# Depthwise convolution by phases: three half-length filters, all four chunks on GpSimd, in a hybrid decoder step on one core

## The reference

```
h = h + 0.5 * SwiGLU_1(rms(h))
n = rms(h);  z = n @ w_in
A: latent attention, 8 heads (prompt: causal; samples: 2048 cached positions in pages)
B: v = u1 * sigmoid(u2)                                        # 512 channels, GLU
   c[t] = conv_b + sum over x = 0..30 of conv_w[x] * v_ext[t + x]   # per channel
   c = silu(layernorm over channels (c))
h = h + concat(A, c) @ w_o
h = h + 0.5 * SwiGLU_2(rms(h))
h = h + sigmoid(rms(h) @ w_pg + b_pg) * (p @ w_pp)
y = rms(h)
```

## Time and profile before

| | |
|---|---|
| median of 3 runs | 2373.71 us (2373.28 to 2376.27) |
| the profiled execution's own time | 2374.75 us |
| its span, first to last instruction | 2372.9 us |
| busy, share of the span | PE 94%, DVE 52%, ACT 25%, POOL 13% |
| mean granted TensorE clock | 0.975 of full speed |

### The profile page before, as it was taken

One profiled execution on the slowest core, in us unless ns is written; L12 is line 12 of the kernel. 1 busy time (PEld: TensorE's weight loads), 2 busy tenths in 40 slices (PEclk: granted clock), 3 DMA queues, 4 the chain that ended last, 5 costly groups with the idle time before them and its releaser, 6 DMA issues.

```text
span 2372.9 us, 36251 instructions
## 1 busy us (share of the span) xinstructions
PE 2235.9 (94%) x14234; PEld 2099.8 (88%) x14234; DVE 1236.1 (52%) x1940; ACT 599.9 (25%) x967; POOL 308.4 (13%) x173
## 2 busy tenths in 40 slices
PE   6999999999999999968888899999999999999897
PEld 5999999999999999735544689999999999999796
DVE  7444444444445725457678546544444444445746
ACT  6211111111112314232342433211111111112423
POOL 0000000000000000799995000000000000000000
PEclk9999999999999999878999999999999999999899
DMA  4111111111111330374343311111111111111202
GB/s 149 45 45 44 44 35 53 53 53 37 50 36 36 131 108 9 102 117 123 113 123 114 110 54 54 36 45 44 39 50 53 53 44 45 35 53 36 80 19 73
DMA packets 97113, 150.84 MB, mean 64 GB/s; under 512 B 12113, under 2 KB 73970, under 8 KB 96610
## 3 DMA queue, kind: packets, MB, share of 16 engines
q1 hardware_dynamic: 96098, 140.49, 19.9%
q0 software_dynamic: 928, 9.17, 1.1%
HBM read 139.21 MB, written 10.42 MB: 63 GB/s over the span
## 4 chain that ended last, share of the span: by engine, by line
PE 81%; DVE 10%; ACT 4%; SPq 2%; issue 2%; DMA 1%; DVEq 0%; ACTq 0%
PE ps L469 25%; PE ps L470 24%; PE ps L471 24%; DVE cacc L1525 2%; PE ps L714 2%; PE ps L671 1%; DVE stat L1628 1%; SPq L322 1%; ACT sq L886 1%; SPq L329 1%; PE ps L729 1%; PE ps L739 1%; DVE n L1278 1%; DVE wlo L1251 1%; PE ps L629 1%
## 5 line engine op out<-in xcount | busy, mean ns | idle before, releaser
L469 PE MATMUL ps<-n_hi,wlo 128*128 128x352 f32 x2832 | 922.8, 326 | 21.6 <-DVE wlo L1251 13.7
L471 PE MATMUL ps<-n_hi,whi 128*128 128x352 f32 x2832 | 911.3, 322 | 0.0
L470 PE MATMUL ps<-n_lo,whi 128*128 128x352 f32 x2832 | 910.9, 322 | 0.0
L469 PEld LDWEIGHTS ps<-n_hi,wlo 128*128 128x128 f32 x2832 | 533.9, 189 | 26.1 <-issue 14.4
L470 PEld LDWEIGHTS ps<-n_lo,whi 128*128 128x128 f32 x2832 | 535.4, 189 | 2.0 <-issue 0.2
L471 PEld LDWEIGHTS ps<-n_hi,whi 128*128 128x128 f32 x2832 | 533.7, 188 | 0.0
L469 PE MATMUL ps<-hid_hi,wlo 128*128 128x352 f32 x1104 | 359.7, 326 | 25.1 <-DVE h L1306 12.1
L470 PE MATMUL ps<-hid_lo,whi 128*128 128x352 f32 x1104 | 355.5, 322 | 0.0
L471 PE MATMUL ps<-hid_hi,whi 128*128 128x352 f32 x1104 | 355.4, 322 | 0.0
L1306 DVE SCALAR_TENSOR_TENSOR h<-ps,h 128x352 f32<-128x352 f32 x552 | 273.1, 520 | 153.1 <-PE ps L471 153.1
L1319 DVE TENSOR_TENSOR gact<-ps,rstd 128x352 f32<-128x352 f32 x132 | 69.1, 523 | 530.9 <-PE ps L471 530.9
(11 more groups left out here) (182 smaller groups left out, 1546.0 us busy)
## 6 DMA issues: line engine op xcount, KB each, us to landing
raw<-in_wstream SPq DMA_DIRECT2D x167, 512.0 KB, 3.6
ttile<-in_cacheT SPq DMA_DIRECT2D x128, 144.0 KB, 2.6
ctile<-in_cache SPq DMA_DIRECT2D x128, 128.0 KB, 2.0
out_yT<-h POOLq DMA_DIRECT2D x1, 4224.0 KB, 13.7
h<-out_yT SPq DMA_DIRECT2D x3, 1408.0 KB, 11.5
out_yT<-n SPq DMA_DIRECT2D x2, 1408.0 KB, 5.7
sw<-in_samplew POOLq DMA_DIRECT2D x1, 2560.0 KB, 10.2
pw<-in_pairw SPq DMA_DIRECT2D x4, 640.0 KB, 4.7
```

Of the source, the lines that this page charges most:

```text
L469: nc.tensor.matmul(out, w_l, x_h, start=first, stop=False)
L470: nc.tensor.matmul(out, w_h, x_l, start=False, stop=False)
L471: return nc.tensor.matmul(out, w_h, x_h, start=False, stop=last)
```

## The change

The prompt's convolution is computed by phases. `vext` and `cacc` keep even and odd positions apart. With E(w) the filter of the 16 even taps on the even positions, O(w) that of the 15 odd taps on the odd ones, and B that of the summed taps on the sum of both phases, the even outputs are E + O, and the odd ones B - E - O shifted by one position. So three filters of half as many positions and about half as many taps replace one of full length. GpSimd does this for all four chunks; VectorE does none of it. VectorE makes the summed taps (`wboth`) and doubled bias (`bias2`) once, and does the samples' convolution in pairs 0, 1, 1 and 2.

Scratch tiles lie in other tiles: the products of chunk 0 in `prod_n` (a part of `n_hi` that `att_high(1)` writes), those of the other chunks in `prod_v` (chunk 0 of `vext`), so GpSimd waits ahead of chunk 1 until SP has stored the prompt's convolution state. That store and the samples' ones move behind load round 5.

The sample queries move in TensorE's list from behind the last GLU tile to behind tile (3, 0), the absorbed ones to behind tile (3, 1); VectorE's scaling and ScalarE's copies move with them. SP loads the page table, the rotary table and the first pair's weights earlier, reads the page numbers of a round before it waits for the round's buffer, and takes the second round's `load_t` ahead of the first `load_c`. GLU, LayerNorm sums, centring and scaling use strided operands; `scale_rows(2)` comes ahead of `conv_low(0)`.

The core of the diff (tiles' places, semaphores and host code are cut):

```diff
-POOL_CHUNKS = (0, 1)
-SHARED, SHARED_DVE, DVE_CHUNK = 2, 17, 3
-POOL_STEPS = len(POOL_CHUNKS) * (2 * TAPS - 1) + 2 * (TAPS - SHARED_DVE)
+HALF = SEQ // 2
+HR, HB = ROWS // 2, RB // 2
+HH, HV = HIST // 2, (HIST + SEQ) // 2
+EVEN = (TAPS + 1) // 2
+FILTERS = [("odd", a) for a in range(1, EVEN)] + [("even", a) for a in range(EVEN)] + [("both", a) for a in range(EVEN)]
+POOL_CHUNK_STEPS = 1 + 2 * len(FILTERS) - 3 + 3
+POOL_STEPS = CC * POOL_CHUNK_STEPS
...
+    zq = scope()
+    phase_p = sb(zq, "phase_p", [P, HV])
+    odd_p = sb(zq, "odd_p", [P, HALF + 1])
+    zq.close()
...
-    vext = sb(zb, "vext", [P, CC, HIST + SEQ])
+    zv = scope()
+    prod_v = sb(zv, "prod_v", [P, HALF + 1])
+    zv.close()
+    vext = sb(zb, "vext", [P, CC, 2, HV])
...
+    prod_n = sb(zo, "prod_n", [P, ROWS])
+    terms_s = sb(zo, "terms_s", [P, ROWS])
...
+    cacc = sb(zo, "cacc", [P, CC, 2, HR])
...
-    product = sqs[:, :, :].rearrange("p c n -> p (c n)")
-
-    def tap_operands(c, x):
-        return (cacc[:, c, 0:SEQ], vext[:, c, x:x + SEQ],
-                gain[:, W_CONV + c * TAPS + x:W_CONV + c * TAPS + x + 1], gain[:, B_CONV + c:B_CONV + c + 1])
+    def half_rows(r):
+        return slice(r * HB, (r + 1) * HB)
+
+    def phases(c, phase, odd, filt, a):
+
+        even, odds, both = vext[:, c, 0], vext[:, c, 1], phase
+        w = W_CONV + c * TAPS
+        if filt == "odd":
+            return odd[:, :], odds[:, a - 1:a + HALF], gain[:, w + 2 * a - 1:w + 2 * a], None
+        if filt == "even":
+            return (cacc[:, c, 0, 0:HALF], even[:, a:a + HALF], gain[:, w + 2 * a:w + 2 * a + 1],
+                    gain[:, B_CONV + c:B_CONV + c + 1])
+        return cacc[:, c, 1, 0:HALF], both[:, a:a + HALF], wboth[:, c, a:a + 1], bias2[:, c:c + 1]
+
+    def by_phase(block):
+        return block.rearrange("p (m two) -> p m two", two=2)
+
+    def glu_rows(c, r, n):
+        return vext[:, c, :, HH + r * HB:HH + r * HB + n].rearrange("p two m -> p m two")
...
+        sp.wait_ge(const_in, 3 * 16)
+        sp.wait_ge(w_split, N_WO)
+        sp.dma_start(ptab[:, :], ptab_d).then_inc(ptab_in, 16)
+        sp.dma_start(tab[:, :], qtrig).then_inc(trig_in, 16)
+        sp.wait_ge(pair_ready, T_WIN + 2 * NRB)
+        sp.dma_start(pw[:, :], pairw[0]).then_inc(pw_in, 16)
+        sp.wait_ge(lat_norm, 2 * NRB)
+        sp.dma_start(ckvT, ckv[:, :, :]).then_inc(out_state, 16)
+        sp.wait_ge(ptab_in, 16)
+        pages = [pages_of(sp, n) for n in range(BUFS)]
         sp.wait_ge(kpe_roped, 1)
         sp.dma_start(kpeT, kpe[:, :]).then_inc(kpe_out, 16)
-        sp.wait_ge(lat_norm, 2 * NRB)
-        sp.dma_start(ckvT, ckv[:, :, :]).then_inc(out_state, 16)
-        sp.wait_ge(pair_ready, T_FF2)
-        sp.dma_start(tab[:, :], qtrig).then_inc(trig_in, 16)
-        sp.dma_start(pw[:, :], pairw[0]).then_inc(pw_in, 16)
         sp.wait_ge(qs_ready, 1)
-        load_t(sp, 0)
+        load_t(sp, 0, pages[0])
         sp.wait_ge(qa_made, 1)
-        load_c(sp, 0)
-        load_t(sp, 1)
-        load_c(sp, 1)
-        sp.wait_ge(hist_in, 16 * CC)
-        sp.wait_ge(pair_free, 2 + T_FF2)
-        sp.dma_start(convp, vext[:, :, SEQ:SEQ + HIST]).then_inc(out_state, 16)
-        for c in range(CC):
-            sp.dma_start(convs[:, c], vs[:, c, :, DEC_T:DEC_T + HIST]).then_inc(out_state, 16)
+        load_t(sp, 1, pages[1])
+        load_c(sp, 0, pages[0])
+        sp.wait_ge(pair_ready, T_WIN + 3 * NRB)
+        load_c(sp, 1, pages[1])
         for n in range(BUFS, LAST + 1):
-            load_t(sp, n)
-            load_c(sp, n)
+            pages = pages_of(sp, n)
+            load_t(sp, n, pages)
+            load_c(sp, n, pages)
+            if n == STEPS + 1:
+                sp.wait_ge(hist_in, 16 * CC)
+                sp.wait_ge(pair_free, 2 + T_FF2)
+                sp.dma_start(convp, vext[:, :, :, HALF:HALF + HH]).then_inc(convp_out, 16)
+                for c in range(CC):
+                    sp.dma_start(convs[:, c], vs[:, c, :, DEC_T:DEC_T + HIST]).then_inc(out_state, 16)
...
@@ -440,26 +472,44 @@
         pool.wait_ge(gain_in, 16)
         pool.wait_ge(lat_norm, 2 * NRB)
         pool.wait_ge(pair_free, 2 + T_FF2)
+        pool.wait_ge(conv_ready, 1)
         done = 0
-        for c, first in [(c, 0) for c in POOL_CHUNKS] + [(SHARED, SHARED_DVE)]:
-            if c == SHARED:
-                pool.wait_ge(conv_half, 1)
-            for x in range(first, TAPS):
-                acc, src, w, b = tap_operands(c, x)
-                if x == 0:
+        for c in range(CC):
+            product = prod_v if c else prod_n
+            if c == 1:
+                pool.wait_ge(convp_out, 16)
+            even, odd = cacc[:, c, 0, 0:HALF], cacc[:, c, 1, 0:HALF]
+            pool.wait_ge(pool_tap, done)
+            nc.gpsimd.tensor_tensor(phase_p[:, :], vext[:, c, 0], vext[:, c, 1], ALU.add).then_inc(pool_tap, 1)
+            done += 1
+            for filt, a in FILTERS:
+                acc, src, w, b = phases(c, phase_p, odd_p, filt, a)
+                pool.wait_ge(pool_tap, done)
+                if (filt, a) == ("odd", 1):
+                    nc.gpsimd.tensor_scalar(acc, src, w, 1.0, ALU.mult, ALU.mult).then_inc(pool_tap, 1)
+                    done += 1
+                    continue
+                if a == 0:
                     nc.gpsimd.tensor_scalar(acc, src, w, b, ALU.mult, ALU.add).then_inc(pool_tap, 1)
                     done += 1
                     continue
-                pool.wait_ge(pool_tap, done)
-                nc.gpsimd.tensor_scalar(product[:, 0:SEQ], src, w, 1.0, ALU.mult, ALU.mult).then_inc(pool_tap, 1)
+                n = HALF + (filt == "odd")
+                nc.gpsimd.tensor_scalar(product[:, 0:n], src, w, 1.0, ALU.mult, ALU.mult).then_inc(pool_tap, 1)
                 pool.wait_ge(pool_tap, done + 1)
-                nc.gpsimd.tensor_tensor(acc, acc, product[:, 0:SEQ], ALU.add).then_inc(pool_tap, 1)
+                nc.gpsimd.tensor_tensor(acc, acc, product[:, 0:n], ALU.add).then_inc(pool_tap, 1)
                 done += 2
+            pool.wait_ge(pool_tap, done)
+            nc.gpsimd.tensor_tensor(odd, odd, even, ALU.subtract).then_inc(pool_tap, 1)
+            pool.wait_ge(pool_tap, done + 1)
+            nc.gpsimd.tensor_tensor(odd, odd, odd_p[:, 1:HALF + 1], ALU.subtract).then_inc(pool_tap, 1)
+            nc.gpsimd.tensor_tensor(even, even, odd_p[:, 0:HALF], ALU.add).then_inc(pool_tap, 1)
+            done += 3
         assert done == POOL_STEPS
 
...
+        def sample_queries():
+
+            pe.wait_ge(const_in, 3 * 16)
+            pe.wait_ge(sw_in, 3 * 16)
+            pe.wait_ge(lat_norm, 2 * NRB)
+            for hd in range(HEADS):
+                for c in range(QC):
+                    w0 = hd % 2 * QC * P + c * P
+                    last = nc.tensor.matmul(ps[:, 7, hd * NEW:(hd + 1) * NEW], sw[:, hd // 2, w0:w0 + P],
+                                            cq[:, c, SEQ:ROWS], start=(c == 0), stop=(c == QC - 1))
+            last.then_inc(qs_made, 1)
...
+        def absorbed_queries():
+
+            pe.wait_ge(qs_ready, 1)
...
+            last.then_inc(qa_made, 1)
...
+                if (c, r) == (CC - 1, 0):
+                    sample_queries()
+                if (c, r) == (CC - 1, 1):
+                    absorbed_queries()
...
-                    last = nc.tensor.matmul(out, sw[0:NOPE, hd // 2, w0:w0 + m], qs[0:NOPE, hd, :], start=True, stop=True)
-        last.then_inc(qa_made, 1)
...
+                if z == 1:
+                    pe.wait_ge(qabs_ready, 1)
                 if z == 2:
-                    pe.wait_ge(new_ready, 1)
...
+                                            lnsq[:, r, c, :] if m else cacc[:, c, :, half_rows(r)],
...
+            if x == CC * NRB - 1:
+                take_absorbed()
...
         def att_high(p):
             act.wait_ge(at_scaled, p + 2)
+            if p == 1:
+                act.wait_ge(pool_tap, POOL_CHUNK_STEPS)
+            if p == 2:
+                act.wait_ge(sample_conv, CC)
...
-            nc.scalar.activation(lnsq[:, r, :, :], cacc[:, :, rows(r)], ACT.Square).then_inc(ln_sq, 1)
+            nc.scalar.activation(lnsq[:, r, :, :].rearrange("p c (two m) -> p c two m", two=2), cacc[:, :, :, half_rows(r)],
+                                 ACT.Square).then_inc(ln_sq, 1)
...
+                v = glu_rows(c, r, HB)
+                nc.vector.tensor_tensor(v, v, by_phase(ps[:, b, 0:RB]), ALU.mult).then_inc(pair_free, 1)
...
+            if x == 3 * NRB:
+                ve.wait_ge(qs_made, 1)
...
+        even, odd = (gain[:, W_CONV:W_CONV + CC * TAPS].rearrange("p (c x) -> p c x", c=CC)[:, :, x:TAPS:2] for x in (0, 1))
+        step.hit(nc.vector.tensor_tensor(wboth[:, :, 1:EVEN], even[:, :, 1:EVEN], odd, ALU.add))
+        step.hit(nc.vector.tensor_copy(wboth[:, :, 0:1], even[:, :, 0:1]))
+        bias = gain[:, B_CONV:B_CONV + CC]
+        step.hit(nc.vector.tensor_tensor(bias2[:, :], bias, bias, ALU.add))
+        step.sync()
```

(79 more changed lines are left out.)

120 lines of the change are left out of this document (41 added, 79 removed).

## The result

The changed kernel takes 2429.11 us in the median of four runs (2428.17 to 2430.5), the kernel before 2373.49 in the same comparison: the ratio is 1.0237 with an interval of 1.0222 to 1.0253, 55.6 us slower. The forecast was 2419 (2390 to 2461). The profiled execution took 2428.17 us, 53.4 more than that of before; its span is 53.3 longer.

The account below looks back on a forecast made before the run. TensorE is busy almost throughout; attention alone sets `conv_done` at 1343.5. With the change GpSimd sets it: 982 + 396 + 7 = 1385, 42 us later, plus 2.7 for the clock; 2374.75 + 45 - 1 = 2419 us, range 2390 to 2461.

Parts of the forecast that it names:

- GpSimd decides, attention is hidden: At `conv_done`: GpSimd's chain ends at 1385, attention no later than about 1323, so attention's gains are hidden.
- The pair's price, 2.08: GpSimd's product and sum at 512 elements: 2.08 us a pair, so 396 us in all (bounds 364 and 444).
- The start, 982: GpSimd's chain waits for the last GLU product, delayed 17 us (12 to 23) by queries, clock and summed filters: start 982.
- The disturbance, 7 us: GpSimd slowed by 11.4 us of VectorE work with both inputs in SBUF: 7 us (bounds 0 and 17).
- the 0.65: GpSimd beside VectorE: 0.65 us lost for each us of VectorE work, from 40 us of disturbance over 62 us.
- full rule: VectorE and GpSimd shut each other out for the whole instruction, which would make the 7 us disturbance 11.
- Attention's end, no later than 1323: Attention: load rounds of 20.5 us from about 955, last issue near 1283, 20 us sooner, ending by about 1323.
- The cold clock, 2.7 us: First LayerNorm sums on TensorE after a 60 us wait: half speed for about 5.4 us, 2.7 lost (bounds 0 and 5).
- `scale_rows` order and the strided passes, nothing: `scale_rows(2)` ahead of `conv_low(0)`, and strided GLU, centring and scaling: costed at 0.
- The hold at chunk 1: Rival: GpSimd waits before chunk 1 for SP's convolution state store; 10 us longer, 2429; chance 0.18.
- Exact halving: Rival: GpSimd's pair price halves exactly to 1.91, early start, hardly disturbed; no change, 2374; chance 0.05.
- hand-overs that vanish: Rival: GpSimd's pair costs 1.73 or less, attention decides at about 1323; 20 us faster, 2353; chance 0.03.

Follow-up runs that it names:

- less30: The changed kernel with 30 of GpSimd's 380 instructions left out (15 pairs of product and sum in chunk 3): 2399.64 us, ratio 1.0106.
- half: The changed kernel with GpSimd's chunks 2 and 3 cut to 7 instructions each of 95: 2324.73 us, ratio 0.9792.
- late: The changed kernel with sample queries, their scaling and the absorbed queries back behind the last GLU tile: 2411.48 us, ratio 1.0159.
- dve3: The changed kernel with chunk 3 of the convolution back on VectorE as 46 taps, GpSimd doing three chunks: 2356.69 us, ratio 0.9929.
- dve3b: dve3 with VectorE's taps ahead of its copies of transposed probabilities, not behind them: 2354.53 us, ratio 0.9921.
- dve3bl: dve3b with the sample and absorbed queries back behind the last GLU tile: 2333.72 us, ratio 0.9837.
- hpages: half with SP again reading each page number twice, one ahead of each transfer: 2342.66 us, ratio 0.9865.
- bpages: The kernel before, with SP reading a round's eight page numbers once, ahead of its transfers: 2371.47 us, ratio 0.9986.

## Why the prediction was right

The forecast was 45 us slower by GpSimd's chain; 55.6 were measured, by that chain. Step by step:

- **GpSimd decides, attention is hidden:** shown by the releaser of L1748, and by less30 and half, which follow the chain's length one for one down to attention's end.
- **The pair's price, 2.08, is the term that was mis-sized.** It was 2.14: the sum took 1.26 us and the product 0.69, in place of about 1.26 and 0.65. So it was the product that was taken too low. Against 2.337 and 1.117 the fixed parts are 2 x 1.26 - 2.34 = 0.18 and 2 x 0.69 - 1.12 = 0.26; the memset's slope had given 0.25 for the product. Four undisturbed chunks are 4 x 101.5 = 406 us where the forecast had 396: 10 of the 11.4 us that GpSimd ended after the forecast 1385.
- **The start, 982:** 982.9. The two query blocks took 6.6 + 8.1 us where 5.4 + 5.5 to 10.9 were counted, and the clock fell behind both. The two tiles behind them took some 2 us longer each than the 7.56 counted (GLU products at 947.82, 963.99 and 981.50). With the summed filters that is 19 us where 17 were taken, but tile (3,0) had ended at 946.74 in place of 948.3: that the start fits to 1 us is in part luck. late shows that this delay reaches the end at full size.
- **The disturbance, 7 us:** 7.4, by the three chunks beside attention against the last one. One reading behind the 0.65 was loose: of the 46 taps, four started after GpSimd's last sum had ended (1279.3; the last at 1295.6), so the same sum gives 0.70 and 8 us. The rate can be checked on dve3, dve3b and dve3bl. Their chains of three chunks took 337.3, 336.3 and 337.1 us against 3 x 101.5; less the 7.4 that the other VectorE work costs, 24 to 25 us were lost to 45 two-input taps of 41 us undisturbed (15 of 1.27 and 30 of 0.74). That is 0.6 us for each us. One tap between a sum and a product of GpSimd's, in dve3, shows how they meet:

```profile
1154.43 1.27 POOL L499 TENSOR_TENSOR cacc<-cacc,prod_v 128x512 f32<-128x512 f32 x1
1154.47 1.77 DVE L1609 SCALAR_TENSOR_TENSOR cacc<-vext,gain,cacc 128x512 f32<-128x512 f32 x1
1155.79 1.01 POOL L497 TENSOR_SCALAR prod_v<-vext,gain 128x512 f32<-128x512 f32 x1
```

  The sum, there first, runs at its full speed to 1155.70; the tap, 0.74 alone, ends 0.54 after that; the product behind it takes 1.01 in place of 0.69. The Trainium skill, "SBUF — State Buffer", "Who interferes with whom", calls the ports that the two engines share an exclusive lock; the trace agrees, with the tap 1.03 us late and the product 0.32. So the loss is shared: VectorE's 45 taps took 58.9 us in dve3 where 41 are undisturbed, 18 lost beside GpSimd's 25. The forecast's "full rule" of 1 us for each us left out that VectorE waits as well.
- **Attention's end, no later than 1323:** it was 1291.5. The bound held and the size was off by 31 us, because the step took SP's round at 20.5 us as it was. With each page number read once, ahead of the transfers, a round takes some 15 where SP doesn't wait; hpages, which reads them as before, ends attention at 1316, close to the forecast. It changed nothing in the time, since all of it is hidden, but it makes the wait 105 us where 60 were forecast.
- **The cold clock, 2.7 us:** the first LayerNorm sums took 9.59 us against 7.34, 2.25 more, and the clock did what the forecast copied from the earlier trace rows. In stretches as above, the end of the wait and what follows:

```profile
1292.00:1396.00 104.00, 0.00 (x0) 0.00 (x0) 0.00 (x0) 0.97 (x2) 95.40 (x98) 0.50 0.00 0
1396.00:1400.00 4.00, 3.23 (x6) 2.01 (x7) 2.36 (x3) 0.00 (x0) 0.43 (x1) 0.50 0.25 66
1400.00:1404.00 4.00, 4.00 (x13) 2.54 (x12) 1.62 (x1) 0.62 (x1) 0.00 (x0) 0.84 0.56 197
```

  But that cost is not shown to be the pause's. The same sums in the changed kernel, in half and in hpages, with TensorE's wait ahead of them:

```profile
1396.77 9.59 PE L873 MATMUL ps<-cacc,ones 128*128 128x352 f32 x24 [106.01 <-DVE stat L1748]
...
1292.38 9.03 PE L874 MATMUL ps<-cacc,ones 128*128 128x352 f32 x24 [1.00 <-DVE stat L1749]
...
1316.36 7.34 PE L874 MATMUL ps<-cacc,ones 128*128 128x352 f32 x24 [1.01 <-DVE stat L1749]
```

  After a wait of 1 us they took 9.03 in half, where the granted clock was 0.61 from 1292 to 1296, and 7.34 in hpages, where it stayed at 1.00. Behind other long waits they took 9.01 (late, 84 us) and 10.37 (less30, 76 us). So what a pause costs there lies between nothing and 3 us. From `conv_done` to the last instruction it was 1029.6 us against 1029.4, and between 1027.0 and 1031.3 in the other runs, with and without a pause ahead of it: of the 2.7, nothing can be shown in the time.
- **`scale_rows` order and the strided passes, nothing:** they are inside the same 1029.6, so they cost nothing that can be seen. The GLU product rose from 0.52 to 0.76 us, under TensorE's tiles but for the last one.
- **The hold at chunk 1** did not occur. SP issued the store at 1053.65, in place of 1078, as its rounds are shorter; chunk 0 ended at 1087.5, and chunk 1 began at 1087.61. That this rival's figure, 2429, is the measured time is chance: the 10 us came from the pair's price.
- **Exact halving, and hand-overs that vanish:** a pair would have had to fall under 1.9; both fall with 2.14, and 0.19 of the 2.14 (less 1.26 and 0.69) are still the two hand-overs.

## What to carry to other kernels

Work moved to an idle engine is free only as long as its chain ends under the cover that it has now, and the same change may shorten that cover: here the chain grew from 314 to 414 us while attention ended 52 us sooner, and the gain of one part paid nothing because of the other. Before work is halved in length and doubled in count, split an instruction's time into a part that scales and a part that doesn't: here 0.26 of the short product's 0.69 us and two hand-overs in each pair stayed. And where two limits lie close together, removing one may show almost nothing (bpages, 4.5 us); test each with the other out of the way, and then share the work out until both end at the same time.

## What the runs showed of the hardware that was not expected

- Reading a page number on SP costs nearly as much as issuing the transfer that uses it, wherever the read stands. Eight `load_t` transfers took 5.9 us without reads between them (bpages) and 10.4 with eight (hpages), so 0.57 for a read and 0.73 for an issue; the eight reads ahead of a round, in the gap between its first transfer and the end of the round before, took 4.6 us or more in every round of bpages from round 2 on, 0.57 each again. By these numbers, and by 128 loads of 0.27 us in place of 256 (above), the shorter round comes from reading each number once and not twice; no run changes the order alone.
- GpSimd's two-input sum of 512 elements has a smaller fixed part (0.18 us) than its scalar product (0.26), worked out from 512 and 1024 elements as above.
- VectorE's GLU product of 352 elements went from 0.52 to 0.76 us when it reads and writes its rows by phases.
